# Prompt attention of a hybrid decoder layer: the reciprocal of the softmax denominators is taken before it is spread, and the second copy of transposed probabilities is issued ahead of it

## The chip, the cores and the metric
One NeuronCore of a Trainium2 chip runs the whole program. The metric is the device time of one execution in microseconds (us), as the median of several runs. Engines are named as the profile names them: PE is TensorE, PEld its weight loads, DVE is VectorE, ACT is ScalarE, POOL is GpSimd, SP is SyncE, which issues most DMAs.

## The reference, cut to what matters
The layer has two branches (windowed attention with sinks, and a spatial gating unit), a merge, and a mixture of experts. The change lies in the attention over the prompt, 1024 tokens in 8 blocks of 128 queries, each of which sees its own and the previous block of keys:

```python
def sink_probs(scores, mask, sinks):
    sc = jnp.where(mask, scores, NEG_INF)
    sink = sinks.astype(jnp.float32).reshape(N_KV_HEADS, Q_GROUP, 1, 1)
    m = jnp.maximum(jnp.max(sc, axis=-1, keepdims=True), sink)
    p = jnp.exp(sc - m)
    denom = jnp.sum(p, axis=-1, keepdims=True) + jnp.exp(sink - m)
    return p / denom
...
def attn_prompt(q, k, v, sinks):
    ...
    p = sink_probs(scores, mask, sinks).astype(vv.dtype)
    o = jnp.einsum("bnkgqs,bnskd->bnqkgd", p, vv).reshape(b, s, ATTN_WIDTH)
```

There are 8 heads of width 64 in 2 key-value groups. So each query has 8 denominators, and its output row has 512 elements.

## The kernel before, in words
The function `attention_phase` writes one instruction stream for each engine by hand. The engines meet only through semaphores; a waiting instruction holds up everything behind it on its own engine. The order of the work is the order in which the code is written, and no scheduler moves anything. A loop over `s` from 1 to 8 is written out in each stream. Pass `s` projects token block `s` to queries, keys and values (three products of rounded high and low parts for each, lines 66 to 68) and finishes the attention of block `done = s - 1`. Block 8, the last, holds the 32 sample tokens. The heads of a block go in two groups of four, `gp` 0 and 1.

PE in a pass: `project_kv(s)`, the scores of the second group, the first half of `project_q(s)`, `probs_turn(done, 0)` (8 transposes of probabilities into PSUM, line 681), a quarter of the projection, `values(done, 0)` (line 695), `probs_turn(done, 1)`, the last quarter of the projection, `values(done, 1)`, `qk_turn(s)` (lines 655 and 656), `dens_turn(done)` (line 708, transposes of the spread reciprocals), `x_turn` of a later block (line 612), and `scores(s, 0)` (line 670).

DVE stands between these: `copy_pT(done, gp)` (line 918) moves the transposed probabilities from PSUM to `pT`, of which there is one buffer, so that `values(done, gp)` can read it. `oa_low` (line 938) makes the low part of an older block's output. `invert_dens` (lines 926 and 927) adds the sinks to the 8 denominators and writes 1/denominator, spread to 64 columns for each head, into `o_sb`, which `dens_turn` transposes. `q_squares` and `k_squares` (lines 859 and 860) sum squares for the norms of queries and keys; POOL makes roots of them (line 367) for `mask_scores` (line 904) and `k_scale`. `copy_kT` (line 891) lets `scores(s, 0)` start. POOL makes `h_low` (line 362) in the middle of a pass. ACT copies queries out of PSUM (line 467), squares them (line 471), takes the exponentials (line 506) and copies `qT` (line 496) and the transposed reciprocals (line 514).

After the loop, the sample tokens' scores (line 723) need `spread_q` (line 971), and the next projection `v_product` needs four weight tiles split by `vs_low` (line 964) on DVE. Later phases begin when this one has ended.

Of the kernel before, what the change touches and what calls it, by code (L numbers as in the profile page):

```python
# [13 lines left out]
P = 128  # L14
# [6 lines left out]
PT = SEQ // P  # L21
NT = PT + 1
HEADS, KV, G, HD = 8, 2, 4, 64
# [27 lines left out]
def rows(t):  # L51

    return P if t < PT else NS
# [62 lines left out]
def attention_phase(nc, io, keep, psum):  # L116
# [7 lines left out]
    with ExitStack() as ctx:  # L124
        def sb(name, shape, dt=F32):
            return ctx.enter_context(nc.sbuf_tensor(name, shape, dt))
# [6 lines left out]
        def sem(name):  # L133
            keep["used"].append(keep["early_semaphores"].enter_context(nc.semaphore("a_" + name)))
            return keep["used"][-1]
# [30 lines left out]
        o_sb = sb("o_sb", [P, G, KV, HD])  # L166
# [15 lines left out]
        rden = sb("rden", [P, 2, G])  # L182
# [43 lines left out]
        rd_made, rT_made, rT_copied = sem("rd_made"), sem("rT_made"), sem("rT_copied")  # L226
# [21 lines left out]
        def k_count(t):  # L248

            return 2 * t + (1 if t < PT else 2)  # L250
# [8 lines left out]
        def block_keys(t):  # L259

            return WIN if t == 0 else 0
# [573 lines left out]
        def _(dve):  # L835
            step = Step(dve, dve_step)

            def mean_square(t):
                n = rows(t)
                dve.wait_ge(x_squared, t + 1)  # L840
                dve.tensor_scalar(xss[0:n, t:t + 1], xss[0:n, t:t + 1], 1.0 / D, EPS, ALU.mult,
                                  ALU.add).then_inc(x_meaned, 1)

            def h_scale(t):
                n = rows(t)
                dve.wait_ge(xT_made, t + 1)
                if t >= 1:
                    dve.wait_ge(h_lo_made, 2 * t)
                for half in range(2):
                    ks = slice(4 * half, 4 * half + 4)  # L850
                    dve.tensor_tensor(h_raw[:, half, :, 0:n],
                                      bank(psum, 6 + half).rearrange("p (k c) -> p k c", k=4)[:, :, 0:n],
                                      g1[:, ks].unsqueeze(2).broadcast_to([P, 4, n]), ALU.mult).then_inc(h_scaled, 1)

            def squares(t, count, heads):
                n = rows(t)
                dve.wait_ge(z_squared, count(t))
                cols = slice(heads.start * HD, heads.stop * HD)
                step.did(dve.tensor_reduce(qks[0:n, heads], z_sq[0:n, cols].rearrange("p (h d) -> p h d", d=HD), AX_X, ALU.add))
                dve.tensor_scalar(qks[0:n, heads], qks[0:n, heads], 1.0 / HD, EPS, ALU.mult, ALU.add).then_inc(z_summed, 1)  # L860

            def k_squares(t):
                squares(t, k_count, slice(HEADS, HEADS + KV))

            def q_squares(t):
                squares(t, q_count, slice(0, HEADS))

            def k_scale(t):
                n = rows(t)
                dve.wait_ge(z_rstd, k_count(t))  # L870
                if t >= 1:
                    dve.wait_ge(qkT_made, t)
                dve.tensor_tensor(k_norm[0:n, :, :], z[0:n, AW:].rearrange("p (k d) -> p k d", d=HD),
                                  qkr[0:n, HEADS:].unsqueeze(2).broadcast_to([n, KV, HD]), ALU.mult).then_inc(k_normed, 1)
                if t == PT:
                    dve.wait_ge(k_out_stored, DMA)
                if t >= PT - 1:
                    dve.wait_ge(k_normed, t + 1)
                    dve.tensor_tensor(k_out[0:n, :, :], k_norm[0:n, :, :],
                                      k_gain[0:n, :].unsqueeze(1).broadcast_to([n, KV, HD]), ALU.mult).then_inc(k_out_made, 1)  # L880

            def sample_q_scale():
                zq = z[0:NS, 0:AW].rearrange("p (h d) -> p h d", d=HD)
                dve.wait_ge(z_rstd, q_count(PT))
                dve.tensor_tensor(zq, zq, qkr[0:NS, 0:HEADS].unsqueeze(2).broadcast_to([NS, HEADS, HD]),
                                  ALU.mult).then_inc(sq_normed, 1)

            def copy_kT(t):
                n = rows(t)
                dve.wait_ge(qkT_made, t + 1)  # L890
                dve.tensor_scalar(kT[:, t, 0:n], bank(psum, 1)[:, KT_AT:KT_AT + n], qk_gain[:, 1:2], None,
                                  ALU.mult).then_inc(kT_copied, 1)

            def mask_scores(t, gp):

                u = 2 * t + gp
                k0 = block_keys(t)
                dve.wait_ge(s_made, u + 1)
                dve.wait_ge(z_rstd, 2 * t + 2)
                if t >= 1:  # L900
                    dve.wait_ge(pT_made, u - 1)
                for kv, i, j, g in heads_of(gp):
                    r, h = g * KV + kv, kv * G + g
                    ins = dve.tensor_tensor_reduce(p_sb[:, gp, j, k0:], scores_bank()[:, j, k0:], mask[:, k0:], qkr[:, r:r + 1],
                                                   sinks[:, h:h + 1], ALU.add, ALU.max, top[:, j:j + 1])
                step.did(ins)
                step.did(dve.tensor_scalar(ntop[:, gp, :], top[:, :], -1.0, None, ALU.mult))
                sink = sinks[:, :].rearrange("p (k a i) -> p a k i", k=KV, a=2)[:, gp]
                dve.tensor_tensor(*(a[:, gp, :].rearrange("p (k i) -> p k i", k=KV) if a is not sink else a
                                    for a in (sink_d, sink, ntop)), ALU.add).then_inc(s_ready, 1)  # L910

            def copy_pT(t, gp):
                u = 2 * t + gp
                dve.wait_ge(pT_made, u + 1)
                if u >= 1:
                    dve.wait_ge(o_made, u)
                first = block_keys(t) // WIN
                dve.tensor_copy(pT[:, first:, :, :].rearrange("p a g c -> p (a g c)"),
                                psum[:, 6 + first:8, :].rearrange("p a c -> p (a c)")).then_inc(pT_copied, 1)

            def invert_dens(t):
                dve.wait_ge(p_made, 2 * t + 2)
                if t >= 1:
                    dve.wait_ge(rT_made, t)
                a, b = (x[:, :, :].rearrange("p a (k i) -> p a k i", i=2) for x in (den, sink_e))
                step.did(dve.tensor_tensor(rden[:, :, :].rearrange("p a (i k) -> p a k i", k=KV), a, b, ALU.add))
                dve.reciprocal(o_sb[:, :, :, :].rearrange("p g k d -> p (g k) d"),
                               rden[:, :, :].rearrange("p a n -> p (a n)").unsqueeze(2).broadcast_to([P, HEADS, HD])).then_inc(rd_made, 1)

            def o_scale(t):  # L930
                dve.wait_ge(o_made, 2 * t + 2)
# [3 lines left out]
            def oa_low(t):  # L935
                dve.wait_ge(oa_hi_made, t + 1)
                src = o_n if t < PT else bank(psum, 4)
                dve.tensor_tensor(oaT[1][:, :, toks(t)],
                                  src.rearrange("p (k c) -> p k c", k=KE)[:, :, 0:rows(t)],
                                  oaT[0][:, :, toks(t)].bitcast(F32), ALU.subtract).then_inc(oa_lo_made, 1)  # L940
# [40 lines left out]
            for s in range(1, NT):  # L981
                done = s - 1
                mask_scores(done, 0)
                if s + 1 < NT:
                    h_scale(s + 1)
                mask_scores(done, 1)
                if s < PT:
                    k_squares(s)
                if s + 2 < NT:
                    mean_square(s + 2)  # L990
                copy_pT(done, 0)
                if s == PT:
                    q_squares(s)
                else:
                    k_scale(s)
                if done >= 1:
                    oa_low(done - 1)
                invert_dens(done)
                if s == PT:
                    k_squares(s)  # L1000
                copy_pT(done, 1)
                if s == PT:
                    sample_q_scale()
                    k_scale(s)
                else:
                    q_squares(s)
                copy_kT(s)
                if s == PT:
                    spread_q()
                    vs_low(0)  # L1010
                o_scale(done)
# [1262 lines left out]
```

## Time and profile before

| | |
|---|---|
| median of 3 runs | 1038.41 us (1037.18 to 1038.84) |
| the profiled execution's own time | 1038.07 us |
| its span, first to last instruction | 1036.1 us |
| PE busy | 927.2 us (89%) |
| DVE busy | 485.4 us (47%) |
| ACT, POOL busy | 362.7 us (35%), 221.1 us (21%) |
| mean granted TensorE clock | 0.943 |
| prompt loop, `s` = 1 to 8 | about 34 to 207 us of the span |
| reciprocal of line 927 | 8 instructions, 3.35 us each |

The span is the distance from the first to the last instruction of one execution; the time of that execution is about 2 us more. The busy share of PE is a mean over the whole program: it says that most phases are bound by the matrix engine, not that each of them is. The granted clock is the share of 2.4 GHz at which TensorE ran, and in a short stretch it is either 1.00 or 0.50.

### The profile page before, as it was taken

Reading aid. Unit: us, or ns where it says so; the run is one execution under the profiler, and the core shown is the slowest. Engines: PE = TensorE matmul, PEld = TensorE weight load, DVE = VectorE, ACT = ScalarE, POOL = GpSimd, SP = SyncE. Lnnn points to the kernel's source line nnn. Section 1 sums busy time; section 2 is a strip of 40 time slices with the busy share of each in tenths; the row PEclk is TensorE's granted clock in tenths of the full one; section 3 lists DMA queues with packets and bytes.
Section 4 is the critical chain, followed back from the end, with each engine's and each line's share of the span. In section 5 each row is a group of like instructions: output and inputs, shape, how many; then the busy total and the mean of one; then the engine's idle time right before and its main releaser. Section 6 shows DMA issues by size and latency. Waiting matters only on the chain. (4 is left out here: it accounts for less than half of the span.)

```text
span 1036.1 us, 15955 instructions
## 1 busy us (share of the span) xinstructions
PE 927.2 (89%) x5277; PEld 826.1 (80%) x5278; DVE 485.4 (47%) x794; ACT 362.7 (35%) x603; POOL 221.1 (21%) x240
## 2 busy tenths in 40 slices
PE   4988888899899999999999989999638999999994
PEld 4766666488699999999999989999626787887873
DVE  4677776544322122222222235344495857666650
ACT  5645443421023211111212132212413757566551
POOL 1423321224412000000000010000112545453642
PEclk9988888889989999999999999999868999999997
DMA  5100111020020111111111014764308797989732
GB/s 204 42 21 21 66 41 47 1 83 1 1 94 1 65 59 33 58 39 52 42 49 48 33 47 144 280 230 146 88 7 339 252 318 244 316 269 303 256 48 41
DMA packets 50926, 114.75 MB, mean 111 GB/s; under 512 B 8205, under 2 KB 26317, under 8 KB 50864
## 3 DMA queue, kind: packets, MB, share of 16 engines
q1 hardware_dynamic: 42352, 96.30, 26.7%
q0 software_dynamic: 7488, 17.85, 7.3%
q8 instruction: 27, 0.44, 0.2%
q10 hardware_dynamic: 1040, 0.00, 0.1%
q14 instruction: 19, 0.16, 0.0%
HBM read 101.57 MB, written 23.00 MB: 120 GB/s over the span
## 5 line engine op out<-in xcount | busy, mean ns | idle before, releaser
L1312 ACT ACTIVATE gate<-psum 128x352 f32<-128x352 f32 x48 | 22.3, 464 | 226.2 <-PE psum L68 226.2
L66 PE MATMUL psum<-w_hi,hT_hi 128*128 128x512 f32 (+3 forms) x216 | 83.8, 388 | 3.8 <-DVE hT_lo L951 3.8
L66 PE MATMUL psum<-hT_hi,x_xT_hi 128*128 x192 | 78.9, 411 | 2.1 <-ACT x_xT_hi L1764 1.1
L67 PE MATMUL psum<-w_lo,hT_hi 128*128 128x512 f32 (+3 forms) x216 | 79.6, 369 | 0.0
L68 PE MATMUL psum<-w_hi,hT_lo 128*128 128x512 f32 (+3 forms) x216 | 79.4, 368 | 0.0
L2010 DVE TENSOR_TENSOR hT_lo<-room,hT_hi (+1 forms) x32 | 71.9, 2288 | 15.9 <-ACT hT_hi L1746 15.9
L66 PE MATMUL psum<-hT_hi,w_hi 128*128 128x352 f32 x240 | 77.4, 323 | 0.0
L67 PE MATMUL psum<-hT_lo,w_hi 128*128 128x352 f32 x240 | 76.9, 321 | 0.0
L68 PE MATMUL psum<-hT_hi,w_lo 128*128 128x352 f32 x240 | 76.9, 320 | 0.0
L67 PE MATMUL psum<-hT_lo,x_xT_hi 128*128 x192 | 76.8, 400 | 0.0
L68 PE MATMUL psum<-hT_hi,x_xT_lo 128*128 x192 | 76.7, 399 | 0.0
L66 PE MATMUL psum<-hT_hi,g_w_hi 128*128 128x352 f32 x192 | 63.3, 330 | 4.5 <-DVE hT_lo L1972 4.5
L67 PE MATMUL psum<-hT_lo,g_w_hi 128*128 128x352 f32 x192 | 62.8, 327 | 0.0
L68 PE MATMUL psum<-hT_hi,g_w_lo 128*128 128x352 f32 x192 | 62.6, 326 | 0.0
L1746 ACT ACTIVATE hT_hi<-room (+1 forms) x32 | 59.7, 1921 | 8.1 <-PE psum L68 7.8
L1367 DVE TENSOR_TENSOR room<-psum,gate 128x352 f32 (+1 forms) x24 | 12.6, 524 | 102.1 <-ACT gate L1312 102.1
L1640 POOL MEMSET c_zeros<- 128x128 f32 x1 | 0.2, 204 | 279.3 <-POOLq L1230 279.3
L66 PE MATMUL psum<-hT_hi,o_w_hi 128*128 128x352 f32 x168 | 54.8, 326 | 2.1 <-DVE yT L1944 2.1
L1367 DVE TENSOR_TENSOR part_b<-psum,gate 128x352 f32<-128x352 f32 x24 | 12.6, 525 | 93.3 <-ACT gate L1312 93.3
L67 PE MATMUL psum<-hT_lo,o_w_hi 128*128 128x352 f32 x168 | 54.5, 325 | 0.0
L68 PE MATMUL psum<-hT_hi,o_w_lo 128*128 128x352 f32 x168 | 54.2, 323 | 0.0
L66 PEld LDWEIGHTS psum<-w_hi,hT_hi 128*128 128x128 f32 (+1 forms) x216 | 41.1, 190 | 15.6 <-issue 9.1
(326 smaller groups left out, 2396.4 us busy)
## 6 DMA issues: line engine op xcount, KB each, us to landing
room<-in_w_gu SPq DMA_DIRECT2D x16, 2048.0 KB, 12.7
dn_raw<-in_w_dn SPq DMA_DIRECT2D x16, 1024.0 KB, 7.4
g_w_raw<-in_w_ab SPq DMA_DIRECT2D x15, 768.0 KB, 4.4
xT_chunk<-in_xT SPq DMA_DIRECT2D x8, 528.0 KB, 3.8
x_in<-in_x SPq DMA_DIRECT2D x8, 512.0 KB, 3.6
out_y<-y SPq DMA_DIRECT2D x8, 512.0 KB, 3.5
hn_rows<-squares SPq DMA_DIRECT2D x8, 512.0 KB, 3.2
o_w_raw<-in_w_out_t SPq DMA_DIRECT2D x7, 512.0 KB, 8.1
```

Of the source, the lines that this page charges most:

```text
L66: eng.matmul(out, lh, rh, start=first and k == 0, stop=False)
L67: eng.matmul(out, lh, rl, start=False, stop=False)
L68: mm = eng.matmul(out, ll, rh, start=False, stop=last and k == nk - 1)
L1312: act.activation(gate[:, (ab + c) % 2, :], bank(psum, pair(ab, c))[:, 0:TC], ACT.Sigmoid).then_inc(gated.sem, 1)
L1367: dve.tensor_tensor(out, bank(psum, pair(ab, c) + 1)[:, 0:TC].unsqueeze(1), gate[:, (ab + c) % 2, :].unsqueeze(1), ALU.mult).then_inc(mult ...
L1640: pool.memset(c["zeros"][:, :], 0.0).then_inc(zeros_made, 1)
L1746: act.activation(gu_hi[:, buf, ks], gu_raw[:, buf, ks], ACT.Copy).then_inc(gu_hi_made.sem, 1)
L2010: dve.tensor_tensor(gu_lo[:, buf, ks], gu_raw[:, buf, ks], gu_hi[:, buf, ks].bitcast(F32), ALU.subtract).then_inc(gu_lo_made.sem, 1)
```

## The change
Two things change in the DVE stream of the prompt loop. `invert_dens` takes the reciprocal of the 8 denominators in place and then spreads them to 512 columns by a copy, where one reciprocal did both. And `copy_pT(done, 1)` moves from behind `oa_low` and `invert_dens` to a place in front of them; in the last pass `k_squares` moves ahead of it with it. No other engine's stream changes.

```diff
@@ invert_dens
                 step.did(dve.tensor_tensor(rden[:, :, :].rearrange("p a (i k) -> p a k i", k=KV), a, b, ALU.add))
-                dve.reciprocal(o_sb[:, :, :, :].rearrange("p g k d -> p (g k) d"),
-                               rden[:, :, :].rearrange("p a n -> p (a n)").unsqueeze(2).broadcast_to([P, HEADS, HD])).then_inc(rd_made, 1)
+                step.did(dve.reciprocal(rden[:, :, :], rden[:, :, :]))
+                dve.tensor_copy(o_sb[:, :, :, :].rearrange("p g k d -> p (g k) d"),
+                                rden[:, :, :].rearrange("p a n -> p (a n)").unsqueeze(2).broadcast_to([P, HEADS, HD])).then_inc(rd_made, 1)
...
@@ the loop over s
                 copy_pT(done, 0)
                 if s == PT:
                     q_squares(s)
+                    k_squares(s)
                 else:
                     k_scale(s)
+                copy_pT(done, 1)
                 if done >= 1:
                     oa_low(done - 1)
                 invert_dens(done)
-                if s == PT:
-                    k_squares(s)
-                copy_pT(done, 1)
                 if s == PT:
                     sample_q_scale()
```

In a middle pass, the stream of DVE from the first copy of probabilities to the squares of the queries reads as follows (- is the kernel before, + the changed one; `pT` is the transposed probabilities, `oaT_lo` the output of `oa_low`, `rden` the 8 denominators, `o_sb` the spread reciprocals).

```order
 L918 COPY pT<-psum 128x1024
 L873 TENSOR_TENSOR k_norm<-z_qkv,qkr 128x128
-L938 TENSOR_TENSOR oaT_lo<-sp_sb,oaT_hi 128x4x128
+L918 COPY pT<-psum 128x1024
+L939 TENSOR_TENSOR oaT_lo<-sp_sb,oaT_hi 128x4x128
 L926 TENSOR_TENSOR rden<-den,sink_e 128x2x2x2
-L927 RECIPROCAL o_sb<-rden 128x512
-L918 COPY pT<-psum 128x1024
+L927 RECIPROCAL rden<-rden 128x8
+L928 COPY o_sb<-rden 128x512
 L859 TENSOR_REDUCE qks<-qkv_w_raw 128x8
```

The second copy of `pT` now stands ahead of `oa_low`, the sum and the reciprocal, and one instruction more stands between the sum and the squares.

In the last pass the same stream reads as follows before, with the squares of the keys (32x2) between the reciprocal and the second copy (`z_qkv` is the scaling of the sample queries):

```order
L859 TENSOR_REDUCE qks<-qkv_w_raw 32x8
L860 TENSOR_SCALAR qks<-qks 32x8
L938 TENSOR_TENSOR oaT_lo<-sp_sb,oaT_hi 128x4x128
L926 TENSOR_TENSOR rden<-den,sink_e 128x2x2x2
L927 RECIPROCAL o_sb<-rden 128x512
L859 TENSOR_REDUCE qks<-qkv_w_raw 32x2
L860 TENSOR_SCALAR qks<-qks 32x2
L918 COPY pT<-psum 128x1024
L885 TENSOR_TENSOR z_qkv<-z_qkv,qkr 32x512
```

and in the changed kernel:

```order
L859 TENSOR_REDUCE qks<-qkv_w_raw 32x8
L860 TENSOR_SCALAR qks<-qks 32x8
L859 TENSOR_REDUCE qks<-qkv_w_raw 32x2
L860 TENSOR_SCALAR qks<-qks 32x2
L918 COPY pT<-psum 128x1024
L939 TENSOR_TENSOR oaT_lo<-sp_sb,oaT_hi 128x4x128
L926 TENSOR_TENSOR rden<-den,sink_e 128x2x2x2
L927 RECIPROCAL rden<-rden 128x8
L928 COPY o_sb<-rden 128x512
L885 TENSOR_TENSOR z_qkv<-z_qkv,qkr 32x512
```

Both squares and the copy of `pT` now come first, and the scaling of the sample queries follows the spreading copy.

## Rows read from the trace of the kernel before

**Rows 1.** Waits of PE in the prompt loop: waiter <- releaser: us, times, longest us

```profile
PE psum L695 <- DVE pT L918: 26.5, 8, 4.0
```

**Rows 2.** PE in one middle pass: start us, length us; in brackets idle before

```profile
103.26 1.08 PE L695 MATMUL psum<-pT,v_ring 128*64 128x256 f32 x8
104.28 1.09 PE L681 MATMUL psum<-ident,sp_sb 128*128 128x128 f32 x8
...
106.37 0.40 PE L68 MATMUL psum<-w_hi,hT_lo 128*128 128x512 f32 x1
...
110.80 1.98 PE L695 MATMUL psum<-pT,v_ring 128*64 128x256 f32 x8 [4.03 <-DVE pT L918]
...
116.52 1.17 PE L670 MATMUL psum<-kT,qT 64*128 64x256 f32 x8
```

**Rows 3.** DVE in the same pass

```profile
103.32 1.79 DVE L938 TENSOR_TENSOR oaT_lo<-sp_sb,oaT_hi 128x512 fp32r<-128x512 f32 x1
105.03 1.25 DVE L926 TENSOR_TENSOR rden<-den,sink_e 128x8 f32<-128x8 f32 x1
106.31 3.35 DVE L927 RECIPROCAL o_sb<-rden 128x512 f32<-128x512 f32 x1
109.58 1.16 DVE L918 COPY pT<-psum 128x1024 f32<-128x1024 f32 x1
```

**Rows 4.** Stretches of the span: length, busy us by engine, PEclk the granted clock

```profile
42.00:47.00 5.00, 3.97 (x32) 3.00 (x32) 3.07 (x7) 3.57 (x7) 2.30 (x4) 1.00 0.20 75
111.00:116.00 5.00, 5.00 (x24) 3.86 (x23) 1.23 (x4) 1.28 (x2) 2.64 (x5) 0.50 0.14 54
209.00:218.00 9.00, 9.00 (x37) 8.06 (x37) 5.50 (x13) 3.22 (x9) 1.62 (x2) 0.50 0.44 118
```

**Rows 5.** PE in the first pass, from the second product of values

```profile
43.07 0.65 PE L695 MATMUL psum<-pT,v_ring 128*64 128x256 f32 x4 [1.03 <-DVE pT L918]
...
44.26 0.60 PE L708 MATMUL psum<-ident,o_sb 128*128 128x128 f32 x4
...
45.66 1.14 PE L670 MATMUL psum<-kT,qT 64*128 64x256 f32 x8
49.77 1.13 PE L670 MATMUL psum<-kT,qT 64*128 64x256 f32 x8
```

**Rows 6.** DVE groups by shape: xcount | busy us, mean ns | idle before

```profile
L851 DVE TENSOR_TENSOR h_raw<-psum,g 128x512 f32<-128x512 f32 x16 | 10.3, 686 | 2.9 <-PE psum L612 2.9
L1037 DVE TENSOR_SCALAR act_v<-act_v,mean_var,rstd 128x512 f32<-128x512 f32 x8 | 4.4, 546 | 5.4 <-POOL rstd L429 5.4
L2059 DVE RECIPROCAL yT<-yT 128x9 f32<-128x9 f32 x1 | 0.2, 215 | 0.0
```

**Rows 7.** DVE in the last pass, `oa_low` while POOL makes no `h_low`

```profile
196.59 0.67 DVE L938 TENSOR_TENSOR oaT_lo<-sp_sb,oaT_hi 128x512 fp32r<-128x512 f32 x1
```

**Rows 8.** ACT and POOL behind the projection of the middle pass

```profile
107.43 0.63 ACT L471 ACTIVATE qkv_w_raw<-z_qkv 128x512 f32<-128x512 f32 x1
...
111.61 1.64 POOL L367 TENSOR_TENSOR qkr<-qks,minus_half 128x8 f32<-128x8 f32 x1 [5.37 <-DVE qks L860]
```

**Rows 9.** PE in the last three passes and at the sample scores

```profile
158.35 1.97 PE L695 MATMUL psum<-pT,v_ring 128*64 128x256 f32 x8 [4.03 <-DVE pT L918]
...
163.35 2.08 PE L670 MATMUL psum<-kT,qT 64*128 64x256 f32 x8
169.49 1.14 PE L670 MATMUL psum<-kT,qT 64*128 64x256 f32 x8
...
181.78 1.97 PE L695 MATMUL psum<-pT,v_ring 128*64 128x256 f32 x8 [2.47 <-DVE pT L918]
...
185.79 1.14 PE L670 MATMUL psum<-kT,qT 64*128 64x256 f32 x8 [0.33 <-ACT qT L496]
...
202.26 1.97 PE L695 MATMUL psum<-pT,v_ring 128*64 128x256 f32 x8 [2.84 <-DVE pT L918]
...
207.63 2.92 PE L723 MATMUL psum<-x_norm,qT_spread 64*128 64x128 f32 x18 [1.87 <-DVE qT_spread L971]
```

## The prediction

> **What bounds the kernel now.** I read the table of waits over the prompt loop first. PE, which the page shows busy for 89% of the span, waits there almost only for one thing: the second product of values waits for the copy of the transposed probabilities, 8 times, 26.5 us in all, 4.0 us at the longest [rows 1]. The timeline of one middle pass shows why. PE ends the 8 transposes of the second group at 104.28 + 1.09 = 105.37 and the last quarter of the projection at 106.37 + 0.40 = 106.77. Then it stands still until 110.80 [rows 2]. In that time DVE finishes `oa_low` (1.79), the sum (1.25) and the reciprocal (3.35), and only then starts the copy that PE waits for, at 109.58 [rows 3]. The copy's input has been ready for 4.2 us. So DVE's order, not its load, sets the end of this stretch.
>
> The second view is the granted clock in the same stretch. After the idle 4 us it is 0.50, the level of 1.2 GHz, from 111 to 116 although PE is busy throughout. In the first pass, where PE stood still for only 1.03 us, it is 1.00 (2.4 GHz) from 42 to 47 [rows 4, 5]. So each long wait is paid twice: once as idle time, and once as slow transposes and scores behind it. From the start of the second product of values to the start of the scores it is 116.52 - 110.80 = 5.72 us in the middle pass [rows 2], and 45.66 - 43.07 = 2.59 us in the first pass, at full clock [rows 5]. The first pass has 4 matmuls of values there instead of 8; for these I add 1.08 - 0.65 = 0.43 [rows 2, 5]. At full clock a middle pass would need 3.02 us, so 2.70 us of each are due to the clock.
>
> **The change part by part.** I count from V, the moment when PE is through with the projection and could start the second product of values (106.77 in the middle pass).
>
> *The moved copy.* Its input is ready at 105.37 = V - 1.4. With 1.16 us for the copy it ends at V - 0.2. PE's wait is gone, all of it: 26.5 us over the 8 passes. DVE now idles some 2 us at the head of the copy, waiting for the transposes; behind it are queued `oa_low`, `invert_dens`, `q_squares` and `copy_kT`.
>
> *Those queued behind it.* `oa_low` starts at V - 0.2. In the old place it took 1.79 us beside `h_low` on POOL [rows 3], in the last pass without it 0.67 [rows 7]; in the new place `h_low` is over, so I take 0.67. The sum, 1.25 in the old place, was held up the same way; it is small, and I take 0.2, as for the reciprocal of 9 elements below. The new reciprocal of 8 elements is nearest to one of 9 elements, 0.215 us [rows 6]. That row also tells that a reciprocal's price goes by the element: 3353 ns for 512 is 6.5 ns each. The spreading copy has no row of its own. From below, it is a single-source operation of 512 elements within SBUF, as `v_normalise`'s is at 0.546 us. From above, an operation of 512 elements with an operand spread by a zero stride, from PSUM, took 0.686 [rows 6]; far above lies 3.35, if it were the spreading that made the reciprocal dear. I take 0.55. The sum is -0.2 + 0.67 + 0.2 + 0.22 + 0.55, and some 0.1 between them: `o_sb` is ready at V + 1.5. PE reaches `dens_turn` at 44.26 - 43.07 + 0.43 = V + 1.62 [rows 5]. So it just does not wait. With 0.69 for the copy it would be V + 1.65, still nothing.
>
> *The chain to the next pass.* At full clock PE ends `scores(s, 0)` at V + 3.02 + 1.14 = V + 4.2 [rows 5]. `mask_scores` also needs POOL's root for the queries: the squares on ACT end at 107.43 + 0.63 = V + 1.3, DVE sums and scales them in the 0.87 us that lie between 109.58 + 1.16 and 111.61, and the root takes 1.64 [rows 3, 8]. That is V + 3.8; behind the spreading copy, which holds DVE until V + 1.5, it is V + 4.0. This wait becomes equal to the scores, and is the one that is late next. It costs nothing if my sum holds, and 0.3 us a pass if it is off by 0.5.
>
> *The clock.* If no wait of several microseconds is left, the clock should stay at 1.00, as in the first pass. This gives back 2.70 us in each of four middle passes (`s` = 2 to 5), 10.6 us with a little less in the first of them. In pass 6 the tail is 163.35 - 158.35 = 5.00 us against about 2.95 (its `x_turn` is short, and the copies of keys and queries set the start), and the scores behind it stretch 169.49 - 163.35 = 6.14 us where the first pass takes 49.77 - 45.66 = 4.11: 4.1 us [rows 5, 9]. Pass 7 has 185.79 - 181.78 = 4.01 against 2.9: 1.1 us [rows 9]. In the last pass PE starts the sample scores 207.63 - 202.26 = 5.37 us behind V + its wait; there the chain over DVE becomes the bound (`o_sb`, then the scaling of sample queries and `k_scale`, about V + 2.7, the turns, and the 1.87 us for `qT_spread`), 5.0 us: 0.4 us [rows 9]. Together 16.2 us.
>
> *The sum.* 26.5 + 16.2 = 42.7 us from the profiled execution's 1038.07: 995.4. The median of the runs shown is 0.34 higher, 1038.41, so 995.7; for small new waits I add 0.3: **996.0 us**. The later phases start when this one ends, and no load issued in the loop is used less than a pass later, so I take the shift as carried to the end.
>
> *A rule that speaks against this.* The row shows the clock low after a wait of 4 us and high after one of 1 us [rows 4, 5]. The Trainium skill, "TensorE: Matmul & The Clock Gate", section "HAM oscillation — how this bites in real kernels", says the same of long waits in a loop: every one brings the clock down again; by that rule the sum is as above. But its section "A second HAM failure mode: psum-queue depth-cycling" says that short idles between groups of matmuls, if frequent, can also make the clock swing; by that rule the 16.2 us would not come. No row here shows such a fall after short idles in the loop.
>
> **The rivals.**
> 1. *The clock falls in the tail all the same.* The tail of a pass is transposes and small products, and waits of tenths of a microsecond remain in it. Then only the waits go: 1038.4 - 26.5 = 1011.9 us. Against it: the first pass has the same tail, with a wait of 1.03 us ahead of it, at 1.00. If only single passes fall, each costs 2.7 us: 996 to 1004.
> 2. *The spreading is what is dear.* If the copy takes 3.35 us as the wide reciprocal did, `o_sb` comes at V + 4.3 and PE waits 2.7 us before `dens_turn` in 8 passes: 21.6 us lost, 1017.6. Against it: the zero-stride operand at 0.686 [rows 6].
> 3. *The sample section runs at full clock too.* Now the clock is 0.50 from 209 to 218 [rows 4], behind the 1.87 us wait for `qT_spread`, which stays [rows 9]. With fewer idles before it, the clock might hold. The scores there would end some 3 us earlier and wait for `vs_low`, and `v_product` would run its first 5 us at twice the speed: about 2.8 us less, 993.2. I count this within my forecast's range, as little speaks for it: the chain with small products is unchanged.
> 4. *Slower.* The second copy now heads DVE's queue, and the reciprocals come after it. They decide when `dens_turn` starts; PE needs 45.66 - 44.26 = 1.40 us from there to the scores, which now start at V + 9.75 (116.52 against 106.77) [rows 2, 5]. So the change loses only if `o_sb` is ready later than V + 8.35, that is if the spreading copy takes over 7.4 us, more than twice the wide reciprocal. With 8 us it would be 0.6 us in 8 passes, about 1043. Nothing points to such a price.
> 5. *Nothing changes*, because the freed time becomes a wait elsewhere of the same length. The only candidates on the path are the root of the queries (V + 4.0) and `o_sb` (V + 1.5), and neither comes near V + 9.75.
>
> **How the numbers follow.** The forecast with its neighbours (rival 3, and single passes that fall) 0.80; rival 1 0.10; rival 2 0.04; something in between 0.02; nothing 0.02; slower 0.02. The range is 991.5 to 1004: below, rival 3's 993.2 less 1.7 for what the clock does later; above, 0.3 us a pass for the root and two to three passes whose clock falls. Rivals 1 and 2 are left out, with 0.14. Runs of this kernel before spread by 1.66 us, and I take 0.2% (2 us) as what a measurement can tell from no change: faster 0.96, same 0.02, slower 0.02.
>
> **What would show it.** In the changed kernel's trace the wait of the second product of values for the copy of `pT` is under 0.3 us in each pass. The granted clock is 1.00 from 40 to about 160. The second products of values stand about 17.0 us apart in the middle passes; before, two passes took from 110.80 to 158.35, 23.8 us each [rows 2, 9]. The reciprocal shows about 0.2 us and the spreading copy about 0.55, and `oa_low` is near 0.67. DVE shows 2 us of waiting for transposes before each second copy. The sample scores start at about 165. I am wrong if the clock is 0.50 somewhere in the loop's tails, if `dens_turn` waits for the spreading copy, or if `mask_scores` waits long for the root of POOL.

## The result, and the profile after

The changed kernel takes 994.14 us in the median of 4 runs (992.42 to 996.66), the kernel before 1037.8 us beside it (1036.25 to 1038.84, 4 runs). The ratio is 0.9583, with a 95% interval of 0.9568 to 0.9598: 4.2% faster. The prediction was 996.0 us, in a range of 991.5 to 1004. The profiled execution took 993.28 us, with a span of 991.3 us and a mean granted clock of 0.964.

The first view is again PE's table of waits over the prompt loop (waiter <- releaser: us in total, times, longest):

```profile
PE psum L723 <- DVE qT_spread L972: 1.7, 1, 1.7
PE psum L695 <- DVE pT L918: 1.3, 1, 1.3
PE psum L670 <- ACT qT L496: 0.4, 1, 0.4
PE psum L708 <- DVE o_sb L928: 0.3, 1, 0.3
```

Of the 26.5 us in 8 waits [rows 1], 1.3 us in one wait are left, in the last pass. Line 708, which reads the spread reciprocals, waits once, for 0.3 us.

PE in two middle passes of the changed kernel (start us, length us), from the second product of values. I call the stretch from there to the first scores the tail of a pass:

```profile
74.44 1.08 PE L695 MATMUL psum<-pT,v_ring 128*64 128x256 f32 x8
75.46 0.66 PE L655 MATMUL psum<-ident,z_qkv 128*128 128x128 f32 x4
76.06 0.60 PE L708 MATMUL psum<-ident,o_sb 128*128 128x128 f32 x4
76.50 1.04 PE L612 MATMUL psum<-ident,x_norm 128*128 128x128 f32 x8
77.47 1.14 PE L670 MATMUL psum<-kT,qT 64*128 64x256 f32 x8
...
91.36 1.08 PE L695 MATMUL psum<-pT,v_ring 128*64 128x256 f32 x8
```

The distance from values to scores is 77.47 - 74.44 = 3.03 us; it was 5.72 [rows 2]. A pass takes 91.36 - 74.44 = 16.92 us; it was 23.8 [rows 2, 9]. DVE in the first of these passes:

```profile
69.71 1.22 DVE L918 COPY pT<-psum 128x1024 f32<-128x1024 f32 x1 [1.06 <-PE psum L681]
70.86 0.28 DVE L873 TENSOR_TENSOR k_norm<-z_qkv,qkr 128x128 f32<-128x128 f32 x1
73.15 1.23 DVE L918 COPY pT<-psum 128x1024 f32<-128x1024 f32 x1 [2.02 <-PE psum L681]
74.29 0.68 DVE L939 TENSOR_TENSOR oaT_lo<-sp_sb,oaT_hi 128x512 fp32r<-128x512 f32 x1
74.89 0.16 DVE L926 TENSOR_TENSOR rden<-den,sink_e 128x8 f32<-128x8 f32 x1
75.09 0.20 DVE L927 RECIPROCAL rden<-rden 128x8 f32<-128x8 f32 x1
75.33 0.43 DVE L928 COPY o_sb<-rden 128x512 f32<-128x512 f32 x1
```

The second copy now waits for the transposes and not the reverse. `oa_low` and the sum, which took 1.79 and 1.25 us beside POOL's work [rows 3], take 0.68 and 0.16. The reciprocal and the spreading copy take 0.63 us together, where the wide reciprocal took 3.35. `o_sb` is ready at 75.76, that is V + 1.3, and PE comes to it at V + 1.6.

The clock in a long stretch of the loop, and behind the loop. Each row gives the stretch, its length, the busy us of PE, PEld, DVE, ACT and POOL, then the granted clock, the share of the DMA engines and GB/s:

```profile
60.00:140.00 80.00, 80.00 (x538) 62.02 (x537) 55.89 (x173) 50.54 (x150) 27.61 (x36) 1.00 0.15 49
```

```profile
166.00:171.00 5.00, 5.00 (x24) 4.65 (x23) 4.71 (x12) 0.29 (x2) 0.00 (x0) 0.50 0.71 207
```

From 60 to 140 us PE is never idle and the clock is 1.00. The low stretch at the sample scores is still there: from 165.4 to 172.2 us here, from 208.8 to 219.0 in the profiled kernel before. Ahead of it PE had only short waits, which the last pass shows (two of 0.29 and 0.18 us lie between these rows):

```profile
159.45 1.08 PE L695 MATMUL psum<-pT,v_ring 128*64 128x256 f32 x8 [1.32 <-DVE pT L918]
...
163.83 2.54 PE L723 MATMUL psum<-x_norm,qT_spread 64*128 64x128 f32 x18 [1.71 <-DVE qT_spread L972]
```

Where the time came from can be read off by three starts: the first transposes of probabilities (line 681), the first sample scores (line 723) and the last small product of the sample values (line 743). Before:

```profile
L681 PE MATMUL psum<-ident,sp_sb x120: 270/272/329, 37.5 to 199.1; 128*128 128x128 f32 x120
L743 PE MATMUL psum<-v_ring,mask x4: 270/294/318, 230.6 to 233.0; 32*128 32x64 f32 x4
```

After:

```profile
L681 PE MATMUL psum<-ident,sp_sb x120: 270/272/329, 36.4 to 157.9; 128*128 128x128 f32 x120
L723 PE MATMUL psum<-x_norm,qT_spread x32: 272/418/579, 163.8 to 168.9; 64*128 64x128 f32 x32
L743 PE MATMUL psum<-v_ring,mask x4: 270/294/318, 185.3 to 187.7; 32*128 32x64 f32 x4
```

The start of the loop came 1.1 us earlier in this execution, ahead of any changed instruction; over the traces of all kernels it lies between 36.4 and 37.5 us, and the kernel before has the latest. The sample scores moved from 207.6 [rows 9] to 163.8, so the loop gave 43.8 - 1.1 = 42.7 us. From there to line 743 another 1.5 us came (45.3 in all), and later phases took 0.5 back: the two profiled executions differ by 44.8 us.

### The profile page after: what moved, and what is told of

Its sections match the earlier page's. It is cut to its first block and busy times, and to the rows that moved or that the text cites. A ratio compares the mean times of both kernels' runs of the same rounds, so it can differ in the third digit from the quotient of the medians.

```text
span 991.3 us, 15963 instructions
## 1 busy us (share of the span) xinstructions
PE 905.4 (91%) x5277; PEld 810.9 (82%) x5278; DVE 453.9 (46%) x802; ACT 362.4 (37%) x603; POOL 218.0 (22%) x240
## 5 line engine op out<-in xcount | busy, mean ns | idle before, releaser
L1683 POOL DMA_INDIRECT out_y<-y,put_at x23 | 39.8, 1732 | 71.4 <-DMA out_y<-y,put_at 61.0
```

Of the source, the lines that this page charges most:

```text
L1683: pool.indirect_dma_start(io["y"], bass.IndirectOffsetOnAxis(put_at[:, j:j + 1], 0), out[:, j, :], None, bounds_check=NTOK - 1, oob_is_err ...
```

## The experiments

Nine kernels were run, each beside the kernel before on the same chip. "Changed" is the changed kernel. The diffs show the lines that matter, and `[...]` in them stands for index expressions that are left out.

**1. The moved copy alone.** The two lines of the reciprocal are taken back, the order is kept.

```diff
-                step.did(dve.reciprocal(rden[:, :, :], rden[:, :, :]))
-                dve.tensor_copy(o_sb[...], rden[...].broadcast_to([P, HEADS, HD])).then_inc(rd_made, 1)
+                dve.reciprocal(o_sb[...], rden[...].broadcast_to([P, HEADS, HD])).then_inc(rd_made, 1)
```

> The copy moved, the wide reciprocal kept. The wait of the second values is gone as in the changed kernel, but the spread reciprocals are ready 3.35 us behind the sum instead of 0.67: about V + 4.1, where V is when TensorE is through with the projection, and TensorE wants them at V + 1.6. Theory (order and price of the reciprocal each matter): a new wait of about 2.5 us before the transposes of line 708 in all 8 passes, so about 994 + 20 = 1014 us if the clock holds at 1.00, up to 1030 if this wait lets it fall. Rival (the order alone was the change): within 2 us of the changed kernel's 994.

Measured: 1022.67 us (1019.83 to 1023.79), ratio 0.9849 (0.9819 to 0.9878). PE's waits in this kernel:

```profile
PE psum L708 <- DVE o_sb L927: 18.0, 8, 3.0
PE psum L723 <- DVE qT_spread L971: 1.7, 1, 1.7
PE psum L695 <- DVE pT L918: 1.3, 1, 1.3
```

The wait moved to the transposes of the reciprocals, 18.0 us in 8 passes, 2.27 us in each of passes 2 to 7. The time is 28.5 us more than changed. The other 10.5 us go with the clock, which was low behind some of these waits and high behind others:

```profile
86.00:89.00 3.00, 3.00 (x14) 2.01 (x12) 0.69 (x1) 1.95 (x4) 2.38 (x5) 0.50 0.00 0
107.00:110.00 3.00, 3.00 (x17) 2.39 (x15) 0.69 (x1) 1.74 (x4) 2.43 (x5) 0.58 0.22 90
126.00:131.00 5.00, 3.97 (x32) 3.42 (x33) 3.96 (x10) 2.27 (x4) 1.64 (x1) 1.00 0.00 0
148.00:153.00 5.00, 5.00 (x23) 4.17 (x23) 3.18 (x13) 0.63 (x1) 0.83 (x1) 0.50 0.34 105
```

So the order alone is worth about a third of the gain. The rival fell.

**2. The narrow reciprocal alone.** The two lines of the reciprocal are put into the kernel before, whose order is kept.

```diff
-                dve.reciprocal(o_sb[...], rden[...].broadcast_to([P, HEADS, HD])).then_inc(rd_made, 1)
+                step.did(dve.reciprocal(rden[:, :, :], rden[:, :, :]))
+                dve.tensor_copy(o_sb[...], rden[...].broadcast_to([P, HEADS, HD])).then_inc(rd_made, 1)
```

> The narrow reciprocal with its spreading copy, and the second copy of probabilities left in its old place. VectorE reaches it 3.35 - 0.65 = 2.7 us earlier, so the wait of the second values shrinks from 4.03 to about 1.35 us in passes 2 to 6. Theory (a wait of this length leaves the clock at 1.00, as 1.03 us did in the first pass): 8 waits of 0 to 1.4 us, about 994 + 9 = 1003 us, clock 1.00 in the tails. Rival (any wait there lets the clock fall): 1003 plus about 2.7 us in each of 6 passes, near 1019.

Measured: 1000.27 us (999.5 to 1001.75), ratio 0.9643 (0.9618 to 0.9669). Its waits and a long stretch:

```profile
PE psum L695 <- DVE pT L918: 8.3, 6, 1.4
```

```profile
60.00:170.00 110.00, 102.25 (x687) 76.47 (x683) 80.57 (x218) 62.08 (x181) 34.46 (x41) 1.00 0.13 41
```

Six waits of about 1.4 us are left, and the clock stays at 1.00. Against the changed kernel's 1.3 us of waits that is 7.0 us more, and the time is 6.1 us more. The narrow reciprocal alone gives 37 of the 43 us.

**3. The changed kernel with a wait of some 2 us put back.** DVE gets unused work ahead of the second copy (written to an array that is not yet in use), so that the copy is late.

```diff
+                for _ in range(6):
+                    step.did(dve.reciprocal(keep["slot_wr"][:, :, :].rearrange("p a s -> p (a s)"), qk_gain[:, 0:1].broadcast_to([P, 2 * PLANNED])))
                 copy_pT(done, 1)
```

> The changed kernel with 6 narrow reciprocals of scratch ahead of the second copy in each pass (about 4.1 us of VectorE's time, 2.1 of which it idled anyway): TensorE waits about 2.0 us for the second values in every pass. Theory (only long waits let the clock fall): 994 + 16 = 1010 us, with the clock at 1.00 in most tails. Rival (a wait of 2 us is long enough): 1010 plus up to 2.7 us in each pass, to 1028.

Measured: 1012.56 us (1011.76 to 1014.1), ratio 0.9756 (0.973 to 0.9781).

```profile
PE psum L695 <- DVE pT L918: 16.7, 8, 4.2
```

```profile
60.00:170.00 110.00, 98.76 (x658) 74.31 (x660) 88.14 (x243) 61.25 (x180) 30.43 (x38) 1.00 0.13 43
```

The waits are 15.4 us longer than in the changed kernel, 1.5 to 2.3 us in passes 1 to 7 and 4.2 in the last. The time is 18.4 us longer. In passes 2 to 6, at 1.7 us each, the clock never fell, nor in pass 7 at 2.3 us; it fell only with the 4.2 us of the last pass.

**4. The same with the wait of before.** Nine of these operations instead of six.

> The same with 9 of them, about 6.1 us: the wait of before, some 4.0 us a pass, put back with everything else of the change kept. Theory (the wait costs twice, itself and the slow tail behind it): 994 + 32 for the waits + about 18 for the clock = 1044 us, clock 0.50 in each middle pass's tail. Rival (the clock's fall has another cause, such as the load of VectorE or the wide reciprocal): 1026 us with the clock at 1.00.

Measured: 1040.92 us (1038.81 to 1046.26, 9 runs), ratio 1.0042 (1.0022 to 1.0061).

```profile
PE psum L695 <- DVE pT L918: 32.3, 8, 6.2
```

```profile
44.00:50.00 6.00, 5.01 (x23) 3.92 (x23) 3.41 (x9) 1.29 (x2) 2.62 (x5) 0.50 0.00 0
90.00:96.00 6.00, 5.94 (x48) 4.87 (x49) 4.76 (x16) 2.85 (x5) 2.62 (x5) 1.00 0.00 1
112.00:116.00 4.00, 4.00 (x23) 3.62 (x23) 1.74 (x5) 1.95 (x3) 2.60 (x5) 0.57 0.16 66
157.00:163.00 6.00, 6.00 (x31) 4.78 (x30) 3.17 (x12) 1.91 (x3) 1.64 (x1) 0.50 0.24 87
```

The waits are 31.0 us longer than in the changed kernel, and the time 46.8 us. The missing 15.8 us go with a low clock in the tails, though DVE has no wide reciprocal here. In the third pass (90 to 96 us) it did not fall. The waits are not quite the old ones: 3.5 to 3.7 us in passes 1 to 6, then 4.3 and 6.2, 32.3 us against 26.5. With waits of this kind put back, the gain is gone.

**5. The kernel before with its wait filled.** The order and the wide reciprocal of before stay. PE computes unused products while it waits, 16 in passes 2 to 6 and in the last (a second call of `fill`, not shown), 10 in pass 7.

```diff
                 project_q(s, 6, KD)
+                fill(s)
                 values(s - 1, 1)
```

> The kernel before, its order and wide reciprocal kept, with 16 unused products on TensorE in the place of the 4 us wait (10 in pass 7, 16 in pass 8, none in pass 1), written to the idle bank of scores. The second values start when they did. Theory (idle time itself lets the clock fall, and that is worth 16 us): clock 1.00 in the tails, and 1038 - 16 = 1022 us. Rival (the tails are slow because VectorE and ScalarE are late, and the clock counts for little there): within 3 us of 1038.

Measured: 1019.57 us (1018.64 to 1019.98), ratio 0.9826 (0.9813 to 0.984); 18.2 us less than the kernel before beside it (1037.73). The clock in the loop:

```profile
60.00:185.00 125.00, 122.53 (x768) 93.46 (x768) 97.70 (x211) 61.28 (x179) 34.10 (x40) 1.00 0.11 37
```

PE in one of its passes:

```profile
83.67 1.08 PE L695 MATMUL psum<-pT,v_ring 128*64 128x256 f32 x8 [0.36 <-DVE pT L924]
...
86.69 1.13 PE L670 MATMUL psum<-kT,qT 64*128 64x256 f32 x8
```

The tail takes 3.02 us, as in the changed kernel, though every instruction of DVE is the one of before. From the first transposes of probabilities (36.5 us) to the sample scores (189.7) it is 153.2 us, and was 170.1 (37.5 to 207.6): 17.0 us of the gain lie in the loop, and most of the rest ahead of it. The rival fell.

**6. The low part ahead of the copy.** `oa_low` returns to the idle 2 us of DVE.

```diff
-                copy_pT(done, 1)
                 if done >= 1:
                     oa_low(done - 1)
+                copy_pT(done, 1)
```

> The changed kernel with the low part of the older block (oa_low) put back in front of the second copy, into the 2 us that VectorE idles there. Beside the work of GpSimd it takes 1.8 us and just fits. Theory (that idle time is free): no change, 994 us within 1.5. Rival (the copy starts late by some tenths in each pass): up to 3 us slower.

Measured: 994.74 us (993.08 to 995.56), ratio 0.9586 (0.9573 to 0.9599), the same as changed. DVE in a middle pass:

```profile
71.21 1.78 DVE L939 TENSOR_TENSOR oaT_lo<-sp_sb,oaT_hi 128x512 fp32r<-128x512 f32 x1
73.31 1.23 DVE L918 COPY pT<-psum 128x1024 f32<-128x1024 f32 x1 [0.32 <-PE psum L681]
```

`oa_low` takes 1.78 us again beside `h_low`, and the copy still starts when the transposes end. DVE's 2 us were free.

**7. The last pass with a cover for its wait.** The projection of keys and values is split around the first product of values; on DVE the squares of the keys go behind the second copy.

```diff
-            project_kv(PT)
+            project_kv(PT, 0, KD // 2)
             values(PT - 1, 0)
             probs_turn(PT - 1, 1)
+            project_kv(PT, KD // 2, KD)
             values(PT - 1, 1)
```

> The changed kernel with the projection of keys and values in the last pass split, one half ahead of each product of values, and the key squares on VectorE behind the copy: there the wait of 1.32 us that the changed kernel still has should be covered. Theory: 1 to 1.5 us faster, 992.8. Rival (the chain behind it over VectorE, k_norm and the spread queries, takes the gain back, since the key squares come later): no change or up to 1 us slower.

Measured: 996.08 us (994.79 to 996.92), ratio 0.9602 (0.9589 to 0.9616), 1.3 us above experiment 6 on the same chip and 1.4 us above the changed kernel's later median (994.72, experiment 9), with ranges that overlap. There is no gain, as the rival had it, for a reason near to the one that it gave. The squares of the keys waited for a projection that now ended later, and held up `oa_low` and the reciprocals behind them on DVE:

```profile
157.26 1.22 DVE L921 COPY pT<-psum 128x1024 f32<-128x1024 f32 x1 [1.62 <-PE psum L683]
159.31 0.27 DVE L862 TENSOR_REDUCE qks<-qkv_w_raw 32x2 f32<-32x128 f32 x1 [0.82 <-ACT qkv_w_raw L483]
159.69 0.67 DVE L942 TENSOR_TENSOR oaT_lo<-sp_sb,oaT_hi 128x512 fp32r<-128x512 f32 x1
```

PE's wait of 1.3 us became one of 1.6 us a step later. The sample scores started 127.6 us behind the first transposes (36.6 to 164.2), as in experiment 9 (36.8 to 164.4). What came on top lies in the low stretch of the clock, which here lasted until 176 us.

**8 and 9. Filler in the last pass, and the changed kernel again.** Unused products on PE ahead of the second values (6), behind them (2) and ahead of the sample scores (8).

```diff
             probs_turn(PT - 1, 1)
+            fill(6)
             values(PT - 1, 1)
+            fill(2)
             dens_turn(PT - 1)
             qk_turn(PT)
+            fill(8)
             sample_scores()
```

> The changed kernel with unused products on TensorE in the short waits of the last pass (6 ahead of the second values, 2 behind them, 8 ahead of the sample scores), to the idle bank of scores. The changed kernel's clock is 0.50 from about 165.3 to 172. Theory (the low clock there comes from TensorE's idle and thin work in the last pass): the clock stays at 1.00 past 172, the sample scores end earlier but v_product still waits for the weights that VectorE splits until about 169.6, so only its first 2.3 us are sped up: 1 to 1.5 us less than the changed kernel's. Rival: the clock falls a little later instead, and the time is the same within 1 us or up to 2 us worse.

> The changed kernel once more, for comparison on the same chip with the one above and with the earlier runs: 994 us within 1.5.

Measured on one chip: 993.5 us with filler (993.41 to 993.77, ratio 0.9579, 0.9566 to 0.9592), 994.72 us without (993.05 to 995.77, ratio 0.9587, 0.9574 to 0.96). The first two rows of the clock are of the kernel with filler, the last of the other:

```profile
165.00:170.00 5.00, 3.81 (x37) 3.70 (x36) 5.00 (x6) 1.83 (x3) 0.00 (x0) 1.00 0.44 144
170.00:172.00 2.00, 1.40 (x3) 1.16 (x4) 1.70 (x9) 0.13 (x1) 0.00 (x0) 0.59 0.57 168
```

```profile
165.00:170.00 5.00, 5.00 (x29) 5.00 (x28) 5.00 (x7) 1.38 (x2) 0.00 (x0) 0.51 0.55 167
```

The filler kept the clock up for the sample scores. They ended early, and PE then waited 1.8 us:

```profile
170.60 0.76 PE L66 MATMUL psum<-w_hi,hT_hi 128*128 128x512 f32 x1 [1.79 <-issue]
```

The row names no releaser, but the kernel waits there for the four split weights, and DVE ends the last of them at 170.51. The clock fell within this wait, at 170.4. The median is 1.2 us lower, but the ranges overlap: whether this beats the changed kernel is not settled.

## Why the prediction was right

**The wait.** The step "PE's wait is gone, all of it: 26.5 us" holds for passes 1 to 7. In the last pass 1.3 us stay. There the copy has no quarter of a projection beside it on PE, since the projection of keys and values comes before; I had applied the middle pass's cover to a pass that has none. The term was too large by 1.3 us, and the sign "under 0.3 us in each pass" failed there.

**The queue behind the copy.** "`o_sb` is ready at V + 1.5" was V + 1.3, since the spreading copy took 0.43 us and not 0.55. The spread operand cost nothing extra, which ends rival 2, and experiment 1 shows the other side: with 3.35 us in this place PE waits 2.25 us for it in each pass. "Nothing, with 0.3 us a pass if off by 0.5" was right as well: `mask_scores` waited for POOL's root 1.3 us in all, in 3 passes, and PE did not wait for `mask_scores`.

**The two halves.** Alone, the narrow reciprocal gives 37 us and the moved copy 15, both together some 43. They shorten the same wait, so they don't add. The prediction did not price them apart.

**The clock.** The 16.2 us were the boldest term. Experiment 5 measures it by itself: the second values start as late behind the projection as before, but PE is kept busy until then, 18.2 us less, of which 17.0 lie in the loop of the profiled execution. Experiment 4 puts the wait back by other means and gets a like loss, 15.8 us over the wait itself. So idle time of PE, not the wide reciprocal and not the load of DVE, took the clock down. Passes 6 and 7 needed 2.76 and 2.65 us from values to scores (127.94 - 125.18 and 144.46 - 141.81), where I had taken 2.95 and 2.9. The last pass needed 4.38 us from the second values to the sample scores (163.83 - 159.45), where I had taken 5.0; this is the most that any part of the term was off. The loop gave 42.7 us, of which 25.2 are waits, so this term came to 17.5 and not 16.2. It made up for the 1.3 us of wait that stayed. That the loop agrees with the sum to 0.1 us is luck in part: two errors that cancel.

**Rival 3** did not come true. The low stretch at the sample scores stayed. In the first trace of the changed kernel it was over at 172.2 us, 2.6 us into `v_product`, where it had reached 5 us into it before; that is the 1.5 us between the sample scores and line 743. But in experiment 9, the same kernel again, it lasted to 175.3 us, and from the sample scores to line 743 it took 23.0 us (164.4 to 187.4), as in the kernel before (207.6 to 230.6). So the 1.5 us are no gain of the change but chance in one execution. This stretch moves from execution to execution, and is at least part of the changed kernel's spread of 4 us.

**Rival 1** fell: no tail in the loop is slow, and one wait of 1.7 us in each of passes 2 to 6 left the clock at 1.00 (experiment 3). The rule on short idles in the Trainium skill, "TensorE: Matmul & The Clock Gate", section "A second HAM failure mode: psum-queue depth-cycling", has no case in these passes. Behind the last pass it is open. There the clock fell at 165.4 us after waits of 1.32, 0.29, 0.18 and 1.71 us, and with unused products put into these waits it held until 170.4 (experiment 8). That speaks for short idles, but the unused products are also larger than the small ones of this pass, and no run tells the two apart.

## What to carry to other kernels

Read the granted clock behind each repeated wait of TensorE, and add what a low clock costs to the wait itself: here 26.5 us of waits cost 43. Where one engine's queue holds both what TensorE wants now and what it wants later, put the first in front, and check each pass of a loop for what covers the copy; the last one often differs. Invert before you spread: the price of a reciprocal goes by its elements.

## What was not expected of the hardware

- The clock's fall is not a matter of the wait's length alone. Waits of 1.7 us never brought it down in five passes (experiment 3), but with one of 1.8 us, behind the small products of the sample scores, it fell (experiment 8). Waits of 2.27 us did in four of the passes 2 to 7 and not in the other two of one execution (experiment 1). Waits of 3.7 us did in passes 2 to 6, except in the third, and with low stretches of different lengths (experiment 4). Waits of 4.0 us did in each of the five passes of the kernel before, and those of 2.5 and 2.8 us in its last two did as well.
- A sum of 8 elements by VectorE took 1.25 us in the old place and 0.16 in the new, where GpSimd's `h_low` is over. In the old place it ended at 106.28 [rows 3], and `h_low` at 106.25, as this row of the kernel before shows:

```profile
103.28 2.97 POOL L362 TENSOR_TENSOR hT_lo<-h_raw,hT_hi 128x512 fp32r<-128x512 f32 x2 [1.03 <-ACT hT_hi L459]
```

The Trainium skill, "GPSIMD Engine Reference", section "1. Specifications", says that VectorE instructions with two inputs in SBUF contend with GpSimd for its SBUF interfaces. The trace agrees for `oa_low` (0.68 alone, 1.78 beside it) and for this sum, which shows that even the smallest such instruction can be held for over a microsecond.
